# The expert turns of a mixture layer at 96 rows instead of 128

## The reference

```python
D_MODEL, N_EXPERTS, TOP_K, D_EXPERT = 1024, 8, 2, 3584

def moe_swiglu(x, w_router, w_in, w_out):
    xt = x.reshape(B * S, D)                       # 256 x 1024
    logits = xt @ w_router
    top_v, top_i = lax.top_k(logits, TOP_K)        # each token picks 2 of 8 experts
    top_w = jax.nn.softmax(top_v, axis=-1)
    gates = sum(one_hot(top_i) * top_w)            # 256 x 8, two entries per row
    for e in range(N_EXPERTS):
        y += gates[:, e] * swiglu(xt, w_in[e], w_out[e])   # 1024 -> 2 x 3584 -> 1024
```

## Time and profile before

| | |
|---|---|
| time, median of 3 runs | 1856.27 us (1856.22 to 1856.33) |
| profiled execution, from its first to its last instruction | 1859.4 us |
| PE busy | 1843.4 us, 99% |
| DVE busy | 1397.7 us, 75% |
| ACT busy | 1199.8 us, 65% |
| POOL busy | 160.6 us, 9% |
| mean granted clock of PE | 0.996 |
| chain of waits, share that is PE | 96% |
| HBM read | 506.8 MB, mean 277 GB/s over the span |

### The profile page before, as it was taken

The page is one execution under the profiler, slowest core; times in us unless marked ns, Lnnn a source line. Parts: engine busy times, 40 slices in busy tenths (PEclk is TensorE's granted clock), DMA queues, the critical chain, the costliest instruction groups (busy, mean ns, idle before and its releaser), DMA issues.

```text
span 1859.4 us, 25694 instructions
## 1 busy us (share of the span) xinstructions
PE 1843.4 (99%) x8848; PEld 1550.7 (83%) x8848; DVE 1397.7 (75%) x1556; ACT 1199.8 (65%) x1344; POOL 160.6 (9%) x184
## 2 busy tenths in 40 slices
PE   9999999999999999999999999999999999999998
PEld 8998888888888888888888888888888888878887
DVE  6666476546677888888888888888889896587653
ACT  6544365437765777677777776777778766666542
POOL 3000000004404400000000000000001221000000
PEclk9999999999999999999999999999999998999999
DMA  9655655554339999999999999999999963445550
GB/s 293 189 179 212 195 181 182 184 198 139 136 129 339 343 395 395 395 395 392 394 395 397 393 394 383 379 385 370 391 376 369 395 259 103 136 148 162 179 197 29
DMA packets 237863, 516.19 MB, mean 278 GB/s; under 512 B 15260, under 2 KB 55312, under 8 KB 237792
## 3 DMA queue, kind: packets, MB, share of 16 engines
q1 hardware_dynamic: 232304, 499.70, 75.0%
q0 software_dynamic: 5184, 14.51, 2.2%
q10 hardware_dynamic: 304, 1.05, 0.2%
HBM read 506.78 MB, written 8.42 MB: 277 GB/s over the span
## 4 chain that ended last, share of the span: by engine, by line
PE 96%; DVE 2%; ACT 1%; issue 0%; DMA 0%; ACTq 0%; DVEq 0%; SPq 0%
PE G L1525 24%; PE G L1527 24%; PE G L1526 24%; PE SM L1527 5%; PE SM L1525 5%; PE SM L1526 5%; PE T L1485 3%; PE T L1929 1%; DVE e_low L718 1%; PE SM L1713 1%; PE G L1796 1%; PE SM L1814 0%; PE SM L1770 0%; PE SM L2073 0%; PE G L1914 0%
## 5 line engine op out<-in xcount | busy, mean ns | idle before, releaser
L718 DVE TENSOR_TENSOR e_low<-e_arrived,e_high 128x2048 fp32r<-128x2048 f32 (+1 forms) x346 | 759.0, 2248 | 86.9 <-ACT e_high L710 86.9
L710 ACT CAST e_high<-e_arrived 128x2048 fp32r<-128x2048 f32 x338 | 624.4, 1913 | 4.8 <-PE SM L1527 4.8
L1525 PE MATMUL G<-e_high,work_r 128*128 128x512 f32 x896 | 353.8, 395 | 1.2 <-DVE e_low L718 0.8
L1527 PE MATMUL G<-e_high,work_r 128*128 128x512 f32 x896 | 349.4, 390 | 0.0
L1526 PE MATMUL G<-e_low,work_r 128*128 128x512 f32 x896 | 348.6, 389 | 0.0
L1525 PE MATMUL G<-dense_high,xT_hi_all 128*128 128x512 f32 (+1 forms) x760 | 295.4, 389 | 1.7 <-ACT work_all L1118 0.7
L1527 PE MATMUL G<-dense_high,xT_lo_all 128*128 128x512 f32 (+1 forms) x760 | 284.1, 374 | 0.0
L1526 PE MATMUL G<-dense_low,xT_hi_all 128*128 128x512 f32 (+1 forms) x760 | 283.1, 373 | 0.0
L492 DVE TENSOR_TENSOR dense_low<-dense_raw,dense_high 128x2048 fp32r<-128x2048 f32 (+1 forms) x73 | 148.0, 2056 | 89.5 <-ACT dense_high L474 88.1
L1527 PEld LDWEIGHTS G<-e_high,work_r 128*128 128x128 f32 x896 | 168.1, 188 | 35.9
L1525 PEld LDWEIGHTS G<-e_high,work_r 128*128 128x128 f32 x896 | 168.3, 188 | 35.4 <-DVE e_low L718 1.7
(11 more groups left out here) (370 smaller groups left out, 2085.9 us busy)
## 6 DMA issues: line engine op xcount, KB each, us to landing
e_arrived<-in_m_w_in_dram SPq DMA_DIRECT2D x448, 512.0 KB, 8.4
e_arrived<-in_m_w_out_dram SPq DMA_DIRECT2D x224, 512.0 KB, 8.2
dense_raw<-in_a_w_in_dram SPq DMA_DIRECT2D x32, 768.0 KB, 6.0
dense_raw<-in_f_w_in_dram SPq DMA_DIRECT2D x44, 512.0 KB, 4.7
dense_raw<-in_w_up_dram SPq DMA_DIRECT2D x16, 1024.0 KB, 5.1
dense_raw<-in_w_down_dram SPq DMA_DIRECT2D x16, 1024.0 KB, 4.9
dense_raw<-in_a_w_out_dram SPq DMA_DIRECT2D x12, 1024.0 KB, 5.1
dense_raw<-in_f_w_out_dram SPq DMA_DIRECT2D x11, 1024.0 KB, 4.9
```

The source lines that it names most:

```text
L710: nc.scalar.copy(e_hi_unit(n), e_raw(n, e_arrived)).then_inc(e_hi, 1)
L718: ins = nc.vector.tensor_tensor(e_raw(n, e_low)[:, at], e_raw(n, e_arrived)[:, at], e_hi_unit(n)[:, at].bitcast(F32), ALU.subtract)
L1525: nc.tensor.matmul(bank, x_hi, w_hi, start=start, stop=False)
L1527: return nc.tensor.matmul(bank, x_lo, w_hi, start=False, stop=stop)
```

## The change

A turn takes `CAP` = 96 slots. The stationary operands of the turns have 96 columns, the results stand on 96 partitions, the copies and splits between them take 4 groups of 96 elements instead of 512 (`slots4`). In the transposes the data has 96 contraction rows and 128 stationary columns, and a 96 x 96 identity passes. Up to three rounds of 8 turns are possible (1 if no expert has more than 96 rows, 2 up to 192, else 3). The weights, their loads and their splits, the number of matmuls in a turn, the indirect DMAs of 128 rows, and the 512 moving columns of each product stay. DVE has one more step in the count of rounds, POOL two more in the placing of slots; the table of slots has 26 blocks of 128 rows instead of 18.

```diff
+CAP = 96
+ROUNDS = -(-S // CAP)
+TURN_BLOCKS = ROUNDS * E + 2
+        def slots4(x):
+            return x.rearrange("p (k s) -> p k s", k=4)[:, :, 0:CAP]
...
 # SP
+                more = sp.value_load(rounds_i[0:1, 0:1], min_val=2, max_val=ROUNDS)
+                with sp.Fori(1, more) as r:
+                    expert_loop(r * E - 1, E, 0)
...
 # POOL
-            steps.then(Q.tensor_scalar(over, pick_rank, float(P), 1.0, ALU.is_gt, ALU.mult))
+            steps.then(Q.tensor_scalar(over, pick_rank, float(CAP), 1.0, ALU.is_gt, ALU.mult))
+            steps.then(Q.tensor_scalar(in_last, pick_rank, float(2 * CAP), 1.0, ALU.is_gt, ALU.mult))
+            steps.then(Q.tensor_tensor(over, over, in_last, ALU.add))
...
 # ACT
-                    nc.scalar.copy(xg_hi[:, half * BANK:(half + 1) * BANK], G[2 + half][:, :]).then_inc(gathered[0], 1)
+                    nc.scalar.copy(slots4(xg_hi[:, half * BANK:(half + 1) * BANK]), slots4(G[2 + half][:, :])).then_inc(gathered[0], 1)
-                nc.scalar.copy(e_hT_hi[:, p % 2, :], T[p % 2][:, :]).then_inc(e_turned_hi, 1)
+                nc.scalar.copy(slots4(e_hT_hi[:, p % 2, :]), slots4(T[p % 2][:, :])).then_inc(e_turned_hi, 1)
-                        nc.scalar.activation(e_silu, G[2 * (s % 2)][:, :], ACT.Silu).then_inc(e_silu_ready, 1)
+                        nc.scalar.activation(e_silu[0:CAP, :], G[2 * (s % 2)][0:CAP, :], ACT.Silu).then_inc(e_silu_ready, 1)
...
 # PE: gather, turn_rows, e_turn, up, down
-                            ins = nc.tensor.matmul(G[2 + half][:, k % 4 * P:(k % 4 + 1) * P], xn[:, c, k * P:(k + 1) * P],
-                                                   pick[:, c, :], ...)
+                            ins = nc.tensor.matmul(G[2 + half][:, k % 4 * P:k % 4 * P + CAP], xn[:, c, k * P:(k + 1) * P],
+                                                   pick[:, c, 0:CAP], ...)
-                    ins = nc.tensor.transpose(G[2 + k // 4][:, k % 4 * P:(k % 4 + 1) * P], xn[:, 0, k * P:(k + 1) * P], ident[:, :])
+                    ins = nc.tensor.transpose(G[2 + k // 4][:, k % 4 * P:k % 4 * P + CAP], xn[0:CAP, 0, k * P:(k + 1) * P], ident[0:CAP, 0:CAP])
-                    ins = nc.tensor.transpose(T[p % 2][:, n * P:(n + 1) * P], e_hid[:, p % 2, n * P:(n + 1) * P], ident[:, :])
+                    ins = nc.tensor.transpose(T[p % 2][:, n * P:n * P + CAP], e_hid[0:CAP, p % 2, n * P:(n + 1) * P], ident[0:CAP, 0:CAP])
-                                ins = three_products(G[2 * (s % 2) + b][:, :], xg_hi[:, k * P:(k + 1) * P],
-                                                     xg_lo[:, k * P:(k + 1) * P], w_hi[:, at], w_lo[:, at], k == 0, k == KD - 1)
+                                ins = three_products(G[2 * (s % 2) + b][0:CAP, :], xg_hi[:, k * P:k * P + CAP],
+                                                     xg_lo[:, k * P:k * P + CAP], w_hi[:, at], w_lo[:, at], k == 0, k == KD - 1)
...
 # DVE
-            steps.then(V.tensor_scalar(roundsf, total, float(P), 1.0, ALU.is_gt, ALU.add))
+            steps.then(V.tensor_scalar(roundsf, total, float(CAP), 1.0, ALU.is_gt, ALU.add))
+            steps.then(V.scalar_tensor_tensor(out=roundsf, in0=total, scalar=float(2 * CAP), in1=roundsf, op0=ALU.is_gt, op1=ALU.add))
-                V.tensor_tensor(e_hT_lo[:, p % 2, :], T[p % 2][:, :], e_hT_hi[:, p % 2, :].bitcast(F32), ALU.subtract
+                V.tensor_tensor(slots4(e_hT_lo[:, p % 2, :]), slots4(T[p % 2][:, :]), slots4(e_hT_hi[:, p % 2, :].bitcast(F32)), ALU.subtract
-                        V.tensor_tensor(e_hid[:, s % 2, :], e_silu, G[2 * (s % 2) + 1][:, :], ALU.mult
+                        V.tensor_tensor(e_hid[0:CAP, s % 2, :], e_silu[0:CAP, :], G[2 * (s % 2) + 1][0:CAP, :], ALU.mult
```

More of the change, by code:

```diff
@@ L937, in _ @@
             pool.wait_ge(rounds_ready, 1)
-            final = pool.value_load(rounds_i[0:1, 1:2], min_val=E - 1, max_val=2 * E - 1)
+            final = pool.value_load(rounds_i[0:1, 1:2], min_val=E - 1, max_val=ROUNDS * E - 1)
             pool.wait_ge(gates_ready, 1)
@@ L954, in _ @@
             picks = lambda x: x.rearrange("p (i c) -> p i c", i=2)
-            steps.then(Q.tensor_scalar(over, pick_rank, float(P), 1.0, ALU.is_gt, ALU.mult))
+            steps.then(Q.tensor_scalar(over, pick_rank, float(CAP), 1.0, ALU.is_gt, ALU.mult))
+            steps.then(Q.tensor_scalar(in_last, pick_rank, float(2 * CAP), 1.0, ALU.is_gt, ALU.mult))
+            steps.then(Q.tensor_tensor(over, over, in_last, ALU.add))
             steps.then(Q.tensor_scalar(turn_no, over, float(E), 0.0, ALU.mult, ALU.add))
             steps.then(Q.tensor_tensor(picks(turn_no), picks(turn_no), topi[:, :, 0:2].rearrange("p c i -> p i c"), ALU.add))
-            steps.then(Q.tensor_scalar(slot_no, over, float(-P), 0.0, ALU.mult, ALU.add))
+            steps.then(Q.tensor_scalar(slot_no, over, float(-CAP), 0.0, ALU.mult, ALU.add))
             steps.then(Q.tensor_tensor(slot_no, slot_no, pick_rank, ALU.add))
@@ L1302, in y_copy @@
                 act.wait_ge(dest_landed, it * 16 + 16)
-                nc.scalar.mul(y_rows[:, b * BANK:(b + 1) * BANK], SM[b][:, :], slot_gate).then_inc(y_copied, 1)
+                nc.scalar.mul(y_rows[0:CAP, b * BANK:(b + 1) * BANK], SM[b][0:CAP, :], slot_gate[0:CAP, :]).then_inc(y_copied, 1)
             gather_copy(0, (0,))
             act.wait_ge(rounds_ready, 1)
-            rounds = act.value_load(rounds_i[0:1, 0:1], min_val=1, max_val=2)
-            last = act.value_load(rounds_i[0:1, 1:2], min_val=E - 1, max_val=2 * E - 1)
+            rounds = act.value_load(rounds_i[0:1, 0:1], min_val=1, max_val=ROUNDS)
+            last = act.value_load(rounds_i[0:1, 1:2], min_val=E - 1, max_val=ROUNDS * E - 1)
             gather_copy(0, (1,))
@@ L1905, in gather @@
                         for k in range(4 * half, 4 * half + 4):
-                            ins = nc.tensor.matmul(G[2 + half][:, k % 4 * P:(k % 4 + 1) * P], xn[:, c, k * P:(k + 1) * P],
-                                                   pick[:, c, :], start=(c == 0 and k % 4 == 0), stop=(c == NT - 1 and k % 4 == 3))
+                            ins = nc.tensor.matmul(G[2 + half][:, k % 4 * P:k % 4 * P + CAP], xn[:, c, k * P:(k + 1) * P],
+                                                   pick[:, c, 0:CAP], start=(c == 0 and k % 4 == 0), stop=(c == NT - 1 and k % 4 == 3))
                     ins.then_inc(gather_full, 1)
@@ L1919, in scatter_bank @@
                 at = slice(b * BANK, (b + 1) * BANK)
-                nc.tensor.matmul(bank[:, :], routeT[:, c * P:(c + 1) * P], y_hi[:, at], start=True, stop=False)
-                nc.tensor.matmul(bank[:, :], routeT[:, c * P:(c + 1) * P], y_lo[:, at], start=False, stop=True
+                nc.tensor.matmul(bank[:, :], routeT[0:CAP, c * P:(c + 1) * P], y_hi[0:CAP, at], start=True, stop=False)
+                nc.tensor.matmul(bank[:, :], routeT[0:CAP, c * P:(c + 1) * P], y_lo[0:CAP, at], start=False, stop=True
                                  ).then_inc(full, 1)
@@ L1938, in _ @@
             pe.wait_ge(rounds_ready, 1)
-            rounds = pe.value_load(rounds_i[0:1, 0:1], min_val=1, max_val=2)
+            rounds = pe.value_load(rounds_i[0:1, 0:1], min_val=1, max_val=ROUNDS)
             with pe.Fori(0, rounds * E) as it:
@@ L2667, in gather_copy @@
                     at = slice(half * BANK, (half + 1) * BANK)
-                    V.tensor_tensor(xg_lo[:, at], G[2 + half][:, :], xg_hi[:, at].bitcast(F32), ALU.subtract
+                    V.tensor_tensor(slots4(xg_lo[:, at]), slots4(G[2 + half][:, :]), slots4(xg_hi[:, at].bitcast(F32)), ALU.subtract
                                     ).then_inc(gathered[1], 1)
@@ L2690, in _ @@
             dve.wait_ge(rounds_ready, 1)
-            rounds = dve.value_load(rounds_i[0:1, 0:1], min_val=1, max_val=2)
+            rounds = dve.value_load(rounds_i[0:1, 0:1], min_val=1, max_val=ROUNDS)
             gather_copy(0, (1,))
```

12 lines of the change are left out of this document (5 added, 7 removed).

## The result

The median went from 1856.42 us (12 runs beside those of the changed kernel) to 1859.98 us (1859.36 to 1864.66). The ratio is 1.0017, 95% interval 1.0010 to 1.0024. The forecast was 1848.4 us and its range ended at 1853.5: wrong, in sign too. In some executions of before, of after and of most other versions PE runs at half clock for about 10 us behind the turns, which makes them some 5 us longer. The profiled execution of before has that stretch, in the last line of the earlier trace rows, and the one of after has not, so its 1859.4 us stand for 1854.3 beside the 1858.6 of after. Of the runs without the stretch before takes 1856.35 us on average and after 1859.85: 3.5 us more.

A forecast was written before the change was run, and what follows sets the result against it. PE, busy 99% of the span, was taken to bound the kernel through distances between its starts. 1859.4 - 7.8 (transposes) - 0.1 (start) = 1851.5 us profiled, 3.1 lower as median: 1848.4 us; range 1834 to 1853.5.

The forecast's parts named there:

- The 4,032 products with 96 stationary columns: taken at nothing.: fp32r products of the expert turns: 0.2265 us each, unchanged with 96 columns; bounds nothing or 13.4 us gained.
- the 13 ns: Fixed part of each fp32r product beside 214 ns for its 512 moving columns, the same at 384 and 512.
- (c): Rival: PE empties the array at 128 shape changes between products and transposes, 22.5 us lost, 1870.9 us; 5%.
- The nearest row, the 2-column transposes: Trace row: transposes with 2 stationary columns cost 0.109 us each, as much as those with 128.
- The 288 transposes: Transposes in the expert turns: moving identity shrinks from 128 to 96 columns, 27 ns less each, 7.8 us gained.
- Does another engine take it back?: Expert turns, each 1.0 us shorter: DVE and ACT have room, transfers a reserve of 3 us a turn.
- The start: Before the turns: extra DVE step, shorter copies and gather; between 0.2 us lost and 1.1 gained, 0.1 gained taken.
- The sum: Whole kernel: 1859.4 - 7.8 - 0.1 = 1851.5 us profiled, 1848.4 us as median.
- (a): Rival: the products' fixed 13 ns go with the stationary columns, 13.4 us more gained, 1835 us; 12%.
- (b): Rival: the transposes in the turns don't get cheaper, or a tighter engine eats the gain, 1856.3 us; 9%.
- (d): Rival: the products' weight load loses a quick form that needs 128 columns, about 400 us slower, 2250; 1%.
- (e): Rival: an expert has over 96 rows, so the loop runs 16 turns, 941 us more, 2789; 2%.

The follow-up runs named there:

- p96_t128: Changed kernel with only its transposes put back to 128 rows and 128 moving columns, products staying at 96 columns; median 1867.55 us, ratio 1.0058.
- p128: Changed kernel with products and the copies before them put back to 128 columns, transposes left at 96; median 1856.21 us, ratio 0.9985; 1851.1 to 1851.5 without half clock.
- p112: p128 with 112 stationary columns in its products; median 1862.41 us, ratio 1.0023; 1857.7 to 1858.1 us without the half-clock stretch.
- p64: Changed kernel with products at 64 stationary columns, slots 64 to 95 not computed; 1858.7 to 1859.1 us without the half-clock stretch, ratio 1.0014.
- spacing: Separate kernel of only matmuls, 36 of each form back to back, nothing of the layer computed; fp32r with 96 columns 230.0 ns apart, with 128 226.6.
- phases: Only matmuls in the kernel's order of operands, 13 forms behind three beginnings; 128 columns at 0 226.7 ns, 96 230.0, stationary block alone at 32 232.6.
- p96_at32: Changed kernel with the 96 stationary columns taken from columns 32 to 127 of each block, not 0 to 95; 1865.87 us, ratio 1.0048.
- before_moved: Kernel before the change with its four stationary buffers moved by 32 columns (128 bytes), nothing else; median 1877.69 us, ratio 1.0120.
- places: Only fp32r matmuls with fixed starts of the stationary and moving blocks; 96 columns from column 32 226.7 ns apart, 128 from column 32 232.6.

## Why the prediction was wrong

By its own steps:

- **"The 4,032 products with 96 stationary columns: taken at nothing."** This is the step that failed. The distance from start to start rose from 227.4 to 230.1 ns in the mean, 10.9 us in all, and p96_t128 has it alone: 1867.55 us. The split into 214 ns for the moving columns and 13 ns fixed was right for 128 columns; the 13 ns were called open, and then bounded by nothing and a gain. The loss had no bound, only a rival of another kind ((c), a drain). The nearest row, the 2-column transposes, was rightly said to say nothing of it, and was then used as the reason against a change all the same. The runs show that at 512 moving columns the fixed part is not a cost that shrinks with the stationary columns but something that varies from 13.3 to 22 ns with count and place, and that nothing undercut 128 columns starting level with the moving block, as before had them.
- **"The 288 transposes": 7.8 us predicted.** Right in kind and nearly in size, in part by luck. The distance within a group fell from 108.5 to 82.9 ns, about the 27 ns that were taken, but there are 224 such gaps and not 288: 5.7 us. Behind the last transpose of each of the 64 groups stands the first product, and the distance from it to the next is 314 ns before and in p128, 303 in p112, 291 after, 285 in p64. It falls there with the load of the product (188, 161 and 134 ns at 128, 96 and 64 columns), but the load alone does not set it: in p96_t128, with the load of 161 ns too, it is 315. What fits all of them is that the longer of two decides, the last transpose's own passing or the load behind it; that is argued from these means, and no run shows it. By the middle turns, times eight, the transposes gave 5.4 us with 128-column products (p128's 117.84 us against 118.52) and 7.3 with 96-column ones (after's 118.97 against p96_t128's 119.88). Most of what the latter has more is 23 ns at each of 64 groups, the one place where the shorter load seems to be worth anything.
- **"Does another engine take it back?"** No, as predicted: PE busy 119.00 of 119 us, no wait for another engine but the 0.6 us at the start. The reserve of the transfers was not tried by the change, as PE did not get faster; p128 tried it with a turn of 117.84 us, and it held.
- **"The start": 0.1 us gained predicted, 0.2 lost measured.** From the gather's start to the end of PE's wait there are 10.63 us before and 10.81 after. The gather lasts 3.76 us against 3.79, so its moving columns don't hold it; that its load does (192 ns in both) fits and is not shown. DVE's extra step costs 0.19 us, as taken.

After, timeline of PE and of DVE:

```profile
575.56 3.76 PE L1916 MATMUL G<-work_all,xn_all 128*128 128x96 f32 x32
...
586.37 0.47 PE L1535 MATMUL G<-e_high,work_r 128*96 128x512 f32 x1 [0.62 <-DVE e_low L724]
```

```profile
577.81 0.16 DVE L2695 SCALAR_TENSOR_TENSOR routing<-routing 128x1 f32<-128x1 f32 x1
578.00 0.15 DVE L2696 CAST rounds_i<-routing 128x1 int32<-128x1 f32 x1
```

- **The sum.** 10.9 - 7.3 + 0.2 = 3.8 us, against 3.5 measured; eight middle turns count a little too much, since the whole stage differs by 3.1. p128: -5.4 + 0.2 = -5.2, measured -5.2.
- **The rivals.** (a) The 13 ns shrink: wrong at 512 moving columns (+3.3 ns in steady stretches for its -3.3), true at 256 (120.1 to 115.9). (b) Transposes not cheaper: refuted, and no engine ate their gain; the products lost more than that. (c) Drain: its direction came out, its cause did not: 231 ns from a product to the first transpose in both kernels, 234 in p128, where it wanted 176 ns more. (d) Quick load lost: refuted, 161 ns for 188. (e) 16 turns: no, 64 transposes of line 1924 are 8 turns.

The rule that was set against the trace, load and matmul together setting the spacing of a stream of pairs, did not hold: the load was 27 ns shorter and the distance 3.3 ns longer. It stands in the Trainium skill, "TensorE: Matmul & The Clock Gate", section "Back-to-back issue gap", which puts such a stream at about 131 ns per matmul of 512 moving columns. Nothing here came under 215.8, with a load beside each. For a matmul by itself that section has another rule: the moving columns at 2.4 GHz and 2.5 ns more, 215.8 ns for 512. That one the trace bears out in the streams of spacing for bf16 (215.8), and for a record of plain fp32 if its columns pass twice (2 x 213.3 + 2.5 = 429.1, measured 429.2); it disagrees for fp32r, where the distance was 226.7 to 235.2. The Trainium skill's rule on the quick weight load, on the same page under "Weight-path perf modes — Fast Weight Load (FWL) and DoubleRow", 128 weights and no FP32, is what spacing shows: a bf16 load lasts 97 ns with 128 columns and 123 with 96, and fp32r has no such step. In the list of PEld (count | busy us, mean ns):

```profile
L93 PEld LDWEIGHTS bank<-wb,xb 128*96 128x96 bf16 x36 | 4.4, 123 | 3.4
...
L93 PEld LDWEIGHTS bank<-wb,xb 128*128 128x128 bf16 x36 | 3.4, 97 | 4.8 <-issue 0.8
```

## What to carry to other kernels

Where PE is full, a change that touches every one of thousands of matmuls is decided by nanoseconds of start-to-start distance: read starts, since mean durations show it as 2 to 3 ns in 390 or, in one list, not at all, and price "nothing" with a loss as well as a gain until a row has that very form. When less of a block is needed, narrow only the operand that passes, and leave the stationary block of an fp32r product with 512 moving columns at 128 columns and starting level, modulo 256 bytes, with the moving block (with 256 moving columns fewer stationary ones were faster here). A bench of matmuls is worth its while only with the kernel's own places and order: phases, which has them, came within 1 ns of the turns of after, p64, p112, p96_at32 and before_moved, spacing and places were up to 5 ns off. Even then a trial in the kernel decides.

## What the runs showed of the hardware that was not expected

- The fixed part of an fp32r product of 512 moving columns is 13.3 ns (226.7) at best, 20 ns (233.4) for 80 or 120 columns or a stationary block that starts 16 columns off, and 22 ns (235.2) for 48 columns; 128 bytes of offset cost the kernel before 21 us, 1.1%. bf16 and plain fp32 show nothing of it between 128 and 96 columns. How load and passing share what they read would be the place to look, but no run here shows the mechanism; nor is it known why (96, 32, 0) has two rhythms.
- Within a group, a plain fp32 transpose costs its moving columns at 2.4 GHz twice over and 2 to 3 ns (108.5 ns for 128, 82.9 for 96), and behind the last one the first fp32r product takes 285 to 315 ns to the next instead of 227 to 230.
- During four groups of four plain fp32 products of 8 moving columns, with three wide products between two groups, the clock fell to half for 10 us in eight of p128's eleven runs, although PE counted as busy from the first group on; with six wide products between them, in none of seven. That is some 5 us, where it falls, for an edit of two lines.
